# Sample-token projections as four array tiles, first head's loads moved forward, k projected once

## What is computed

```python
h = rmsnorm(x, norm_mix_w)
proj = h @ w_in      # dq,dk,dv,dz (8x128 each), db,da (8 each), sq (1024), sk,sv (128 each), gate_a,gate_b (1024 each)
o_a = deltanet_branch(dq, dk, dv, dz, db, da, conv_buf, s0, ...)   # 4-tap causal conv, gated delta rule in chunks
o_b = swa(sq, sk, sv, dist, valid, sinks, rel_bias)                 # 16 query heads, 2 kv heads, window 128
mixed = sigmoid(gate_a) * o_a + sigmoid(gate_b) * o_b
x = x + mixed @ w_out
x = x + hier_moe(rmsnorm(x, norm_ffn_w), ...)                       # 64 experts of 1024x256, top 2
```

## Time and profile before

| | |
|---|---|
| time, median of 3 runs | 1822.44 us (1820.24 to 1826.62) |
| time of the profiled execution | 1823.06 us |
| its span, first to last instruction | 1821.1 us |
| mean granted TensorE clock | 0.90 |
| TensorE busy | 1509.3 us, 83% |
| VectorE busy | 810.8 us, 45% |
| ScalarE busy | 331.8 us, 18% |
| start, loop, after the loop | 0 to 89.5, 89.5 to 1054.8, 1054.8 to 1821.1 us |

### The profile page before, as it was taken

How to read it: one execution, slowest core, us unless ns; L and a number is a source line. 1 busy time by engine, 2 the same in 40 slices (tenths; PEclk the granted TensorE clock), 3 DMA queues, 4 the chain that set the end, 5 groups by cost and what they waited for, 6 DMA issues and landing times.

```text
span 1821.1 us, 20925 instructions
## 1 busy us (share of the span) xinstructions
PE 1509.3 (83%) x6916; PEld 869.5 (48%) x6916; DVE 810.8 (45%) x1700; ACT 331.8 (18%) x887; POOL 199.6 (11%) x301
## 2 busy tenths in 40 slices
PE   6698998998999989999999879728877777787880
PEld 5456757556566575575665754323222222222220
DVE  1156376565673765656737632342221221221224
ACT  3112222122131221221212220101111110110112
POOL 2201110111011110110111100021000000000002
PEclk9889999899998998998989969958898898988995
DMA  7922011030110110301101232037999999999995
GB/s 158 245 57 52 25 48 35 24 82 24 47 35 24 48 35 24 82 24 47 35 24 24 104 114 84 25 140 278 423 421 423 421 422 423 421 422 422 422 408 182
DMA packets 130366, 307.66 MB, mean 169 GB/s; under 512 B 19708, under 2 KB 92374, under 8 KB 105366
## 3 DMA queue, kind: packets, MB, share of 16 engines
q1 hardware_dynamic: 116934, 263.06, 39.6%
q0 software_dynamic: 8800, 27.52, 4.2%
q10 hardware_dynamic: 4608, 16.78, 2.3%
HBM read 273.50 MB, written 34.83 MB: 169 GB/s over the span
## 4 chain that ended last, share of the span: by engine, by line
PE 62%; DMA 22%; DVE 6%; issue 4%; ACT 4%; SPq 2%; POOL 0%; ACTq 0%; DVEq 0%; POOLq 0%
DMA arena<-in_w_up 20%; PE PB L1049 14%; PE PB L1066 11%; PE PB L1383 7%; PE PB L1072 5%; PE PB L1055 4%; PE PB L1327 4%; PE PB L1183 2%; PE PB L1155 1%; PE PB L1012 1%; DVE arena L1541 1%; PE PB L1092 1%; PE PB L1258 1%; PE PB L1267 1%; PE PB L1021 1%
## 5 line engine op out<-in xcount | busy, mean ns | idle before, releaser
L1383 PE MATMUL PB<-arena 128*64 128x512 f32 x1024 | 269.6, 675 | 113.7 <-DMA arena<-in_w_up 109.8
L1049 PE MATMUL PB<-arena 128*128 128x512 f32 x512 | 258.5, 669 | 0.0
L1066 PE MATMUL PB<-arena 128*128 128x384 f32 (+1 forms) x640 | 213.6, 487 | 0.0
L1383 PEld LDWEIGHTS PB<-arena 128*64 128x64 f32 x1024 | 76.6, 154 | 281.2 <-issue 143.1
L1867 DVE TENSOR_SCALAR arena<-arena 128x256 f32<-128x256 f32 x32 | 9.4, 295 | 381.9 <-ACT arena L928 381.9
L1049 PEld LDWEIGHTS PB<-arena 128*128 128x128 f32 x512 | 109.4, 217 | 136.8 <-issue 136.5
L1072 PE MATMUL PB<-arena 128*128 128x128 f32 x1280 | 156.9, 277 | 2.4 <-ACT arena L815 2.4
L1072 PEld LDWEIGHTS PB<-arena 128*128 128x128 f32 x1280 | 149.2, 192 | 7.0 <-ACT arena L815 3.2
L1066 PEld LDWEIGHTS PB<-arena 128*128 128x128 f32 (+1 forms) x640 | 108.9, 174 | 88.3 <-issue 29.0
L877 ACT ACTIVATE arena<-PB 128x512 f32<-128x512 f32 (+3 forms) x116 | 60.0, 521 | 481.2 <-PE PB L1391 253.8
L1403 PE MATMUL PB<-arena 128*64 128x512 f32 x512 | 116.9, 598 | 1.1 <-ACT arena L877 1.1
(11 more groups left out here) (396 smaller groups left out, 1788.0 us busy)
## 6 DMA issues: line engine op xcount, KB each, us to landing
arena<-in_w_gate SPq DMA_DIRECT2D x64, 1024.0 KB, 19.4
arena<-in_w_up SPq DMA_DIRECT2D x64, 1024.0 KB, 21.5
arena<-in_w_down SPq DMA_DIRECT2D x64, 1024.0 KB, 25.3
arena<-in_w_in SPq DMA_DIRECT2D x56, 512.0 KB, 5.4
ye_d<-arena ACTq DMA_DIRECT2D x32, 512.0 KB, 8.2
ye_d<-mixed SPq DMA_DIRECT2D x2, 2048.0 KB, 15.6
Sb<-in_state_dn SPq DMA_DIRECT2D x8, 512.0 KB, 4.0
out<-Sb POOLq DMA_DIRECT2D x8, 512.0 KB, 3.9
```

What stands on the lines that cost most here:

```text
L1049: last = mm(PB[g][:, :], wch[:, c, g, :], hT[:, c, 0:TP], start=c == 0, stop=c == KC - 1)
L1066: last = mm(PB[5 + n % 2][0:R, 0:3 * P], hT[:, c, n * P:n * P + R], wrow[:, c, :, :].rearrange("p g k -> p (g k)"), start=c == 0, stop=c = ...
L1383: last = mm(gu_bank[a][half[k], :], xT[:, a, c, half[k]], wgu[a][:, k, :, c, :], start=c == 0, stop=c == KC - 1)
```

## The change

Five parts.

1. **Sample tokens in four tiles.** At the head of each head's turn, 32 matmuls take the 32 sample tokens as stationary operand and let the weights stream: each chunk has four matmuls into the four 32-partition groups of `PB[6]`, 192 and 192 columns (z and the two gates) and 256 and 256 columns (q with v, k with sq). They replace L1055 and the fifth rows tile. ScalarE copies the q, v, k, sq part to `srow`, and two transposes turn it to where L1055 wrote. `gate_mul` and the exponential of the sample tile come first in the head (`gate_rows`), the other tiles swap banks. TensorE now waits for `wrow` at the head's start.
2. **Order of the sample chain.** Its first transposes and L1121 come after `square(1)`, and `scores(0)`, `square(2)` come before L1194; on VectorE `powt(1)`, `softmax(0)` and `powt(2)` move likewise. `gate_mul(4)`, which stood between `powt(1)` and `softmax(0)`, now handles prompt tile 3 and stands before `Tt`.
3. **First head's loads.** `wkd` is gone, so the first head's convolution rows and `wch` are queued right after the small loads, ahead of the bias table; `wrow` and the state follow when `wbk` has been read. `rel_d` is written from ScalarE's queue, from memory in `orow`. The bias comes after the first head's loads, the fill of `ye_d` after the bias, read from it. VectorE waits for the bias at its softmax, not ahead of the loop.
4. **k once.** One 128-channel projection of both kv heads; ScalarE copies the halves that are at their place (4 copies, 6 before), VectorE the halves that move to the other 64 partitions (8 copies).
5. **k rows where needed.** L1012's products have 144 columns (db, da, v), and 272 for the last prompt tile; the sample tile comes first, with 272 columns as well.

```diff
-            for u in range(2):
-                for v in range(2):
-                    sp.dma_start(wkd[:, :, v, u, :], w_r[:, :, C_SK + v * HD:C_SK + (v + 1) * HD]).then_inc(s_wkd_in, 16)
...
+            conv_rows(0)
+            channel_weights(0)
+            sp.wait_ge(s_kd_ps, 1)
+            sp.wait_ge(s_bk_ps, NT)
+            row_weights(0)
+            sp.wait_ge(s_stored, 1)
+            states(0)
+            sp.wait_ge(s_rel_out, 16)
+            sp.dma_start(bias, bass.AP(rel_d.tensor, 127, [[383, P], [P * 384, SH], [1, 256]])).then_inc(s_bias_in, 16)
...
+            act.dma_start(rel_d, relr.unsqueeze(1).to_broadcast([SH, P, 384])).then_inc(s_rel_out, 16)
...
             pe.wait_ge(s_rel_done, 1)
...
+            for c in range(KC):
+                mm(PB[5][:, 0:TS], wk(c), hT[:, c, TP:T], start=c == 0, stop=c == KC - 1)
+            for c in range(KC):
+                last = mm(PB[4][:, :], wk(c), hT[:, c, 0:TP], start=c == 0, stop=c == KC - 1)
...
                 pe.wait_ge(s_wch_in, h * 64 + 64)
+                pe.wait_ge(s_wrow_in, h * 48 + 48)
                 pe.wait_ge(s_o_done, 1 + h * NT)
+                for c in range(KC):
+                    xs = hT[:, c, TP:T]
+                    wr_ = wrow[:, c, :, :].rearrange("p g k -> p (g k)")
+                    first, end = c == 0, c == KC - 1
+                    mm(PB[6][0:32, 0:192], xs, wr_[:, 0:192], start=first, stop=end)
+                    mm(PB[6][32:64, 0:192], xs, wr_[:, 192:384], start=first, stop=end)
+                    mm(PB[6][64:96, 0:256], xs, wch[:, c, 0:4:2, :], start=first, stop=end)
+                    last = mm(PB[6][96:128, 0:256], xs, wch[:, c, 1:4:2, :], start=first, stop=end)
...
-                        for k in range(4):
-                            for c in range(KC):
-                                last = mm(PB[4][:, k * TS:(k + 1) * TS], wch[:, c, k, :], hT[:, c, TP:T], start=c == 0, stop=c == KC - 1)
+                        pe.wait_ge(s_raw_done, h * 8 + 1)
+                        pe.sem_inc(s_pe_passed, 1)
+                        for k in range(2):
+                            last = tr(PB[4][:, 64 * k:64 * k + 64], srow[HD:P, k, :], ident[HD:P, HD:P])
...
-                rows(4)
...
                 square(1)
+                pe.wait_ge(s_rows_done, 1 + h * NT + NT)
+                tr(b6[0:TS, 224:352], ks_, ident[:, :])
+                tr(b6[0:TS, 352:480], co[:, 2, TP:T], ident[:, :]).then_inc(s_smp_ps, 1)
                 pe.wait_ge(s_gm_ready, h * 2 + 2)
-
+                pe.sem_inc(s_pe_passed, 1)
+                mm(b6[0:TS, 0:TS], sS[:, 8, 0:TS], s_gt[:, :], start=True, stop=True).then_inc(s_smp_ps, 1)
+                scores(0)
+                square(2)
                 pe.wait_ge(s_smp_done, h * 13 + 5)
...
-            dve.wait_ge(s_bias_in, 48)
+            dve.wait_ge(s_kd_ps, 1)
+            for q in range(2):
+                lo, hi = slice(32 * q, 32 * q + 32), slice(HD + 32 * q, HD + 32 * q + 32)
+                cp(kz[hi, 1, 0, :], PB[4][lo, :]).then_inc(s_kd_done, 1)
+                cp(kz[lo, 0, 1, :], PB[4][hi, :]).then_inc(s_kd_done, 1)
+                cp(skd[hi, 0, :], PB[5][lo, 0:TS]).then_inc(s_kd_done, 1)
+                cp(skd[lo, 1, :], PB[5][hi, 0:TS]).then_inc(s_kd_done, 1)
```

More of the change, by code:

```diff
@@ L174, in program @@
         sig = sb("sig", [P, 2, 3, P])
+        srow = sb("srow", [P, 2, P])
         Sb = sb("Sb", [P, B, P])
@@ L450, in program @@
         LV = 6
+        gate_rows = (NP, *range(NP))
+        gate_bank = (PB[6], PB[5])
         @block.sync
@@ L470, in _, with channel_weights @@
             sp.dma_start(rtab[33:34, :], sinks.unsqueeze(0)).then_inc(s_rel_in, 16)
-            sp.wait_ge(s_rel_done, 1)
-            sp.dma_start(rel_d, relr.unsqueeze(1).to_broadcast([SH, P, 384])).then_inc(s_rel_out, 16)
+            st_r = conv_state.rearrange("b s (g k) -> (b s) g k", g=3)
+            cw_r = conv_w.rearrange("s (g k) -> s g k", g=3)
+            def channel_weights(h):
+                for g, c0 in enumerate((0, GATE_W, 2 * GATE_W, C_SQ)):
+                    sp.dma_start(wch[:, :, g, :], w_r[:, :, ds(h * P + c0, P)]).then_inc(s_wch_in, 16)
@@ new lines, in conv_rows, with row_weights, states @@
+            def conv_rows(h):
+                sp.dma_start(cs[0:24, :, :], st_r[:, :, ds(h * P, P)]).then_inc(s_cs_in, 16)
+                sp.dma_start(cs[24:28, :, :], cw_r[:, :, ds(h * P, P)]).then_inc(s_cs_in, 16)
+            def row_weights(h):
+                for g, c0 in enumerate((C_Z, C_GA, C_GB)):
+                    sp.dma_start(wrow[:, :, g, :], w_r[:, :, ds(h * P + c0, P)]).then_inc(s_wrow_in, 16)
+            def states(h):
+                sp.dma_start(Sb[:, :, :], dn_state.rearrange("b h k v -> h k b v")[ds(h), :, :, :].rearrange("a k b v -> (a k) b v")).then_inc(s_st_in, 16)
@@ L479, in _ @@
-            sp.wait_ge(s_kd_ps, 2)
-            sp.wait_ge(s_bk_ps, NT)
-            with sp.Fori(0, H) as h:
+                sp.dma_start(ye_rows[:, NPAIR + k * NP:NPAIR + (k + 1) * NP, :], bias.rearrange("p (a r) k -> p a (r k)", a=NP)).then_inc(s_bias_in, 16)
+            with sp.Fori(1, H) as h:
                 sp.wait_ge(s_proj_ps, 1 + h * 4)
-                for g, c0 in enumerate((0, GATE_W, 2 * GATE_W, C_SQ)):
-                    sp.dma_start(wch[:, :, g, :], w_r[:, :, ds(h * P + c0, P)]).then_inc(s_wch_in, 16)
+                channel_weights(h)
@@ L485, in _ @@
                 sp.wait_ge(s_cst_ps, 1 + h)
[L486 to L492 removed]
+                conv_rows(h)
@@ L1196, in _ @@
                 tr(b6[0:TS, 96:128], sS[:, 3, 32:64], ident[0:TS, 0:TS]).then_inc(s_smp_ps, 1)
-                scores(0)
-                square(2)
                 grow(1)
@@ L1507, in _, with gate_mul @@
                 cp(hbeta[:, :], scal[:, 0, :, ds(h)].rearrange("p n k -> p (n k)")).then_inc(s_hs_ready, 1)
+                def gate_mul(i):
+                    n = gate_rows[i]
+                    R = rows_of[n]
+                    dve.wait_ge(s_rows_exp, h * (NT + 1) + (i + 2))
+                    s = sig[0:R, i % 2, :, :]
+                    if i == 0:
+                        sf = sig[:, 0, :, :].rearrange("p g k -> p (g k)")
+                        ch.inc(ts(sf[0:32, 0:192], sf[0:32, 0:192], 1.0, None, ALU.add))
+                        step(ts(sf[0:32, 192:384], sf[32:64, 0:192], 1.0, None, ALU.add))
+                    else:
+                        step(ts(s, s, 1.0, None, ALU.add))
+                    step(dve.reciprocal(gates[0:R, n, :, :], s))
+                    tt(gates[0:R, n, 0, :], gates[0:R, n, 0, :], gate_bank[i % 2][0:R, 0:P], ALU.mult).then_inc(s_rows_done, 1)
+                gate_mul(0)
                 w = lambda g, i: cst[:, g, 24 + i:25 + i]
@@ L1533, in _ @@
                     tt(co[:, g, :], co[:, g, :], ex[:, g, :], ALU.mult).then_inc(s_co_done, 1)
-                def gate_mul(n):
-                    R = rows_of[n]
-                    dve.wait_ge(s_rows_exp, h * NT + (n + 1))
-                    b = PB[5 + n % 2]
-                    s = sig[0:R, n % 2, :, :]
-                    step(ts(s, s, 1.0, None, ALU.add))
-                    step(dve.reciprocal(gates[0:R, n, :, :], s))
-                    tt(gates[0:R, n, 0, :], gates[0:R, n, 0, :], b[0:R, 0:P], ALU.mult).then_inc(s_rows_done, 1)
-                gate_mul(0)
                 gate_mul(1)
+                gate_mul(2)
                 dve.wait_ge(s_rn_done, h * 2 + 2)
@@ L1552, in _ @@
                 tt(Rv, v4(3), bc(0), ALU.mult).then_inc(s_kvr_done, 1)
-                gate_mul(2)
+                gate_mul(3)
                 dve.wait_ge(s_Em_ready, h * 2 + 2)
@@ L1607, in _ @@
                 powt(1)
-                gate_mul(4)
+                b6 = PB[6]
+                dve.wait_ge(s_sE_exp, h + 1)
+                sp_ = lambda k: hbeta[0:TS, NP:NT] if k == 0 else hsc[0:TS, k, NP:NT]
+                ts(sS[:, 0, :], b6[0:TS, 352:480], sp_(0), None, ALU.mult).then_inc(s_smp_done, 1)
+                ts(sS[:, 1, :], b6[0:TS, 224:352], sp_(2), None, ALU.mult).then_inc(s_smp_done, 1)
+                ts(sS[:, 2, :], b6[0:TS, 224:352], sp_(4), None, ALU.mult).then_inc(s_smp_done, 1)
+                tt(sS[:, 3, 32:64], sS[:, 3, 0:TS], s_ge[:, :], ALU.mult).then_inc(s_smp_done, 1)
+                tt(sS[:, 3, 64:96], sS[:, 3, 0:TS], s_gt[:, :], ALU.mult).then_inc(s_smp_done, 1)
                 softmax(0)
+                powt(2)
                 dve.wait_ge(s_smp_ps, h * 11 + 3)
@@ L1615, in _ @@
                 tt(sS[:, 4, 64:96], b6[0:TS, 64:96], sS[:, 4, 32:64], ALU.mult).then_inc(s_smp_done, 1)
-                powt(2)
                 growt(1)
```

144 lines of the change are left out of this document (67 added, 77 removed).

## The result

| | before | after |
|---|---|---|
| time, median of 4 runs each | 1822.22 us (1820.24 to 1826.62) | 1718.4 us (1714.72 to 1719.78) |
| span of the profiled execution | 1821.1 us | 1717.2 us |
| mean granted TensorE clock | 0.900 | 0.901 |
| first tile product, or first L1049 | 89.51 us | 71.42 us |
| loop, to the first instruction behind it | 965.26 us | 878.35 us |

The ratio is 0.9424, 95% interval 0.9401 to 0.9447: faster by 5.8%. Forecast were 1697 us and 1678 to 1740. The mean clock is the first thing to see. It did not rise, though the change was to take away the place where it fell.

The account below looks back on a forecast made before the run. TensorE was taken to bound the loop of heads, the weight stream the end. From 1823.06 us, 105 for the loop and 20.5 for the start came off: 1697.6, or 1697 against the median; range 1678 to 1740.

Parts of the forecast that it names:

- The loop: Loop of eight heads: 13.1 us saved per head, 105 us in all.
- the start: Before the first head: first tile matmul at 69 against 89.51 for the first L1049, 20.5 us saved; bounds 65.5 and 73.
- The four tiles: Sample tokens' stage at each head's start: four tiles run together, 4.0 us per head, bounds 3.4 and 6.9; in series 12.0.
- the slow start: Low clock around each head's start, 2.2 us per head, 18 in all: left as it is, beginning before the tiles.
- Transposes and turns of mode: Two 64-column transposes and turning the array to tiles and back: 0.5 us added per head.
- The order: Sample chain, fifth rows tile gone: L1202 comes 6.0 us earlier per head, bounds 3.2 to 7.5; new TensorE gap 1.7.
- VectorE at the convolution: Convolution chain behind a faster TensorE: 0.7 us short of binding, priced at nothing, upper bound 1 us per head.
- The clock: Low-clock stretch from L1055 into L1049 goes: 4.5 us per head, 36 in all.
- rival (a): Low clock stays, brought down once per head by the tile stage or solve stage: +4.5 x 8, 1733 us; chance 0.16.

Follow-up runs that it names:

- e1: Changed kernel with the tile stage ordered by tile (8 chunks of one tile, then the next) instead of by chunk: 1761.24 us.
- e2: Changed kernel with the tile stage done twice, the second time over the first: 1745.22 us.
- e10: Changed kernel with three idle 512-column products a head, one ahead of the 8-column products, two behind the head's last product: 1692.85 us, ratio 0.9284.
- e9: Changed kernel with the sample chain's order put back as before on TensorE and VectorE, the fifth rows tile still gone: 1741.6 us.
- e3: Changed kernel with the 32 narrow products of before put back after the q projection, their result overwritten: 1796.87 us.
- e5: Changed kernel with the k projection computed twice into the same banks before it is signalled: 1725.75 us.
- e6: Changed kernel with one idle 512-column product a head ahead of the 8-column products: 1708.37 us, ratio 0.9366.
- e8: Changed kernel with two idle 512-column products behind each head's last product: 1702.77 us, ratio 0.935.
- e7: Changed kernel with one idle 512-column product a head between the last projection and the first rows tile: 1697.96, 1706.09, 1721.21 and 1731.07 us.
- e11: e10 with wbk in memory of its own, so the first head's row weights are issued straight behind its channel weights: 1689.8 us, ratio 0.9265.
- e4: Changed kernel with the start's load order as before (rel_d from SyncE's queue, bias, fill of ye_d, then first head's weights), k projected once: 1733.24 us.

## Why the prediction was right, and what it mis-sized

The sign, the mechanism and the range held; the time came out 21 us above the forecast. The loop gave 86.9 us where 105 were due, the start 18.1 where 20.5 were due, and the part behind the loop took 1.1 us longer.

**The four tiles** were right. In series they take 11.8 us (e1, 12.0 forecast), together 3.45 for a set more (e2) or 3.59 in place (e10), where I took 4.0 between 3.4 and 6.9. L1284, at half clock, was a good witness for the form. In the changed kernel the stage lasts 4.86 to 6.41 us, since it runs under the head's low clock. I had named that bound and had left the slow start where it was, ahead of the tiles. It reaches over them.

**Transposes and turns of mode**, 0.5: L1088 takes 0.34, and the turns at most about 0.1 behind the tiles (e2).

**The order** gave 17.15 - 10.99 = 6.2 against 6.0. The new gap in front of L1218 is 1.50 us (1.7 forecast), and L1202's 16.5 us of waiting are gone. With the new stage it needs the new order (e9).

**VectorE at the convolution**, priced at nothing: TensorE waits for no VectorE line there. Its two waits for ScalarE in that part grew by 0.7 and 3.1 us over the whole loop, L1125's to 6.3 from 5.6 and L1105's to 5.5 from 2.4.

**The clock was the mis-sized term.** I had counted 36 us behind L1055 as gone and 18 at the heads' starts as staying, and had taken it that a fall that goes does not come back elsewhere. The 36 were right for the place: e3 brings the stretch back with the narrow products. They were wrong for the loop: its summed loss fell from 54.6 to 46.9 us and not to 18. This is rival (a) in part: it named the solve stage as a place where the clock may fall, at 4.5 a head. It fell at that stage's end, behind the 8-column products, for 1.7, and took the rest in longer stretches at the heads' starts and in head 0.

That nothing else was off by much shows in e10, whose loop at a clock of 1.00 is 853.8 us. Of this, 24 idle products take 24 x 0.86 = 20.6. The waits that they fill were 10.3 us in front of L1065 and 1.9 in front of the loop's end (4.56 in the changed kernel, 2.7 in e10). Without both the loop would last 853.8 - 20.6 + 12.2 = 845.4, and 841.6 if the 3.8 us of low clock that are left in e10 count in full. The forecast's loop, 965.26 - 105 = 860.3, with its 18 us of low clock left out, is 842.3, so all other terms together are off by 3 us at most. The low clock then costs 33 to 37 us of the changed kernel's loop (less than the 46.9, since TensorE also waits in those stretches). That is 15 to 19 above my 18, and the loop missed by 105 - 86.9 = 18.1.

**The start** missed by 2.4 us. L1038, k and the copies came as worked out (65.76 against 65.5). The row weights' three issues took 5.82 us where 2.53 were assumed, and landed at 71.4 instead of 68.6. The write of `rel_d` was then under way in ScalarE's queue, until about 62.8 us, and e5, where it had ended, has the loads 4.6 us shorter; I had kept a shared DMA as the upper bound of 73. By the Trainium skill (DMA: Bandwidth & Descriptors, Arbitration), where an engine alternates between the queues by packets, I had estimated 73. The trace, 71.4, lies between my 69 and that.

**Open** stays what makes the clock fall where it does. It falls where the narrow products stand (e3) and not there without them. With a wide idle product ahead of the 8-column products or of a head's start it does not fall at that place (e6, e8, e10). But the kernel before has the 8-column products without a fall, and in e7 they have one in some heads and none in others. That the idle product works by keeping TensorE busy there, and not by shifting what follows, is therefore likely and not shown. A rule that would have told the 164-to-189 stretch of head 0 in advance does not follow from these runs.

## What to carry to other kernels

Where few tokens meet many weights, the tokens belong on the stationary side, four 32-row groups in turn, neighbours always in different groups: with 32 tokens, 3.45 us instead of 11.8 for the same instructions. Count the clock's loss as a sum over the whole stage, not by place: when one fall is removed, part of it can come back elsewhere. Here 36 us of falls were removed and the whole loss shrank by 7.7. Where TensorE waits anyway, a wide idle product in the gap is worth a try: 24 of them, 20.6 us of work, made this kernel 25.5 us faster.

## What the runs showed of the hardware that was not expected

- More work made the kernel faster: one, two and three idle products a head gave 1708.37, 1702.77 and 1692.85 us, against 1718.4 without. They stood at places chosen by the trace (e6, e8, e10); one a head at a place where no clock falls gave 1697.96 to 1731.07 (e7).
- The runs of one kernel spread by 2%, in step with their mean granted clock (0.919 to 0.893), where low-clock stretches remain: 1697.96 to 1731.07 us (e7), against 1689.19 to 1691.43 where the clock is nearly whole (e11).
- Within one tile stage the four groups move at their own pace. At half clock a 192-column tile takes its next instruction after 0.32 us and a 256-column one after 0.43. The short ones end first, and the stage lasts as long as the long ones, 16 x 0.43 = 6.9 us at half clock.
- SyncE's time to issue the same three loads was 2.43 us once the 3 MB write was over and 5.82 beside it, and in e4 the four `wch` loads (L476) took 17.49 us behind the fill of `ye_d`, against 8.37 in the changed kernel. Issuing is slower in the runs where other transfers are under way; no run isolates the cause.
